# Compressed branch with the token blocks stationary and built by GpSimd, and the rotations' exchanged rows copied inside SBUF

## The chip, the cores and the metric

The kernel runs on one core of a Trainium2 chip. The metric is device microseconds of one execution. A few names are used throughout. PE is TensorE, DVE is VectorE, ACT is ScalarE, POOL is GpSimd and SP is SyncE, which here only issues DMA transfers. SBUF is the on-chip memory of 128 partitions, PSUM the memory into which TensorE writes; GpSimd works in SBUF only here. "Slab" is a 1024 x 256 piece of a weight matrix, "block" its half of 128 output columns.

## What is computed

Two transformer-like blocks over 512 tokens and 1024 channels. The second one has a sparse attention with three branches, a gated linear attention (GLA) and a merge by sigmoid gates. The change touches two places of it: the compressed branch, in which windows of 32 tokens (step 16, so 31 windows) become one key and one value through a small network, and the rotation of queries and keys.

```python
def compress_blocks(kv, pe, w1, w2):          # kv: b, g=2, t=512, d=64
    sub = kv.reshape(b, g, n_sub, CMP_STRIDE, d)
    blocks = jnp.concatenate([sub[:, :, r:r + n_cmp] for r in range(ratio)], axis=3)
    blocks = (blocks + pe).reshape(b, g, n_cmp, CMP_LEN * d)
    return jax.nn.silu(blocks @ w1) @ w2      # 2048 -> 128 -> 64

def partial_rope(x, pos):                     # half = 8 of 64 channels
    x1 = x[..., :half]
    x2 = x[..., half:ROPE_DIM]
    return jnp.concatenate([x1 * cos - x2 * sin, x2 * cos + x1 * sin, x[..., ROPE_DIM:]], axis=-1)
```

The compressed keys then give scores with the unrotated queries, a softmax, and probabilities that are multiplied with the compressed values.

## The kernel before

Everything is written out by hand: each engine has its own list of instructions, and semaphores order them. Activations lie transposed, channels in partitions and the 512 tokens along the free axis. Every large product is done three times at reduced precision (hi*hi, hi*lo, lo*hi), so one block of 128 output channels is 24 products 128x512 (L446). SP loads a slab (w_raw, L343), ACT copies its high part (w_hi, L979), DVE subtracts for the low part (w_lo, L1452); a ring of two slabs is used. PE puts the blocks into four PSUM banks in turn, and block n waits until block n-4 has been emptied. Four other banks, misc 0 to 3, serve small products; `take(b)` waits until the last contents of bank b have been read.

In the stretch that matters here the large products are the eight blocks of the merge gate b, slabs 12 to 15 of the second block's input projection, called block 0 to 7 below. They don't depend on the attention and are put between its small products, so that PE has work while DVE, ACT and POOL finish other steps. ACT empties each with a tanh (gate_out, L1181).

PE's order before: GLA outputs, blocks 0 and 1, mean squares, block 2, spread of the roots (L774), block 3, four rotation products (L783), block 4, two rotation products, block 5, the hidden layer of the compressed branch (L793), block 6, compressed keys (L800) and values (L805), mask and scores (L812, L818), block 7, transposition of the probabilities (L827), then the attention steps, with the blocks of gate a between them.

A rotation takes a constant 128x128 matrix (rot) that exchanges 8 rows with 8 others and turns signs. For each of six tiles (two of keys, four of queries) PE multiplies it, POOL multiplies the tile with cos (L2125), DVE multiplies the PSUM result with sin (L1858) and adds both (L1861). Between the fourth and fifth pair DVE does four ob_lo operations of the GLA output (L1853).

For the hidden layer the windows tile holds, for keys and values and both groups, the raw channels in partitions 0 to 63 (DVE, L1864) and the same shifted by one token in 64 to 127 (ACT, L1298), and the position terms in extra columns (POOL, L2128). Each of 32 products has 128x128 weights as stationary and 66 moving columns at a step of 16 tokens; two of the 66 give the position bias, which DVE adds afterwards (L1871, L1873). ACT does the tanh (L1303), DVE the product (L1877).

ACT's order in the stretch: GLA squares and roots, split of slab 14, four ob_hi, gate_out 0 to 3, four window copies, split of slab 15, two tanh (behind ob_lo), gate_out 4 and 5, split of slab 16, exponentials of the scores. POOL's: two DMA issues for the second weights when the GLA outputs are there (L2118), the cos products, the position columns, a memset, and nothing until the attention steps. A float32 product shows as two records on PE, a large one (reduced precision) as one.

Of the kernel before, what the change touches and what calls it, by code (L numbers as in the profile page):

```python
# [25 lines left out]
P = 128  # L26
# [55 lines left out]
def constants():  # L82
# [9 lines left out]
    rot = np.zeros((P, P), f)  # L92
    for base in (0, HD):
        for k in range(half):
            cos[base + k] = cos[base + half + k] = np.cos(ang[k])
            sin[base + k] = sin[base + half + k] = np.sin(ang[k])
            rot[base + half + k, base + k] = -1.0
            rot[base + k, base + half + k] = 1.0
# [12 lines left out]
    return {"c_recip": recip.reshape(P, -1), "c_cos": cos, "c_sin": sin, "c_rot": rot,  # L111
# [4 lines left out]
def build(nc, a, out):  # L116
# [25 lines left out]
    ROT = at("rot", [P], f32, CB + 3.5)  # L142
# [117 lines left out]
    CONST_DMAS = 5  # L260
# [16 lines left out]
    RS4 = at("gla_roots", [T], f32, R1 + 55)  # L277
# [7 lines left out]
    RAWC = at("kv_cmp_raw", [2, T], f32, R1 + 82)  # L285
    COS, SIN = at("cos", [T], f32, SB + 8), at("sin", [T], f32, R1 + 86)
    OBHI, OBLO = at("ob_hi", [4, T], f32r, R1 + 40), at("ob_lo", [4, T], f32r, R1 + 48)
    Z = at("cmp_windows", [4, T + 32], f32, R1 + 56)
    VBD = at("v_cmp_blocks", [2, 4 * HD], f32, R1 + 82)
    W2 = [at(f"cmp_w2_{i}", [HD], f32, CB + 6 + 0.25 * i) for i in range(2)]  # L290
    HX = [at(f"cmp_hidden{i}", [2 * 32], f32, R1 + 64.5 + 0.25 * i) for i in range(2)]
    HT = [at(f"cmp_tanh{i}", [2 * 32], f32, R1 + 65 + 0.25 * i) for i in range(2)]
    HB = at("cmp_bias", [2], f32, R1 + 65.5)
    KC = at("k_cmp", [32], f32, R1 + 65.625)
# [31 lines left out]
    def _(sp):  # L326
# [31 lines left out]
        for c in range(CC):  # L358
# [3 lines left out]
            if c == 1:  # L362
                for dst, src in [(RECIP[:], a["c_recip"].rearrange("p (g n) -> p g n", n=16)),
                                 (ROT[:], a["c_rot"]), (CAUS32[:], a["c_causal"]),
# [35 lines left out]
        for j, q in enumerate((2, 3, 0, 1)):  # L400
            load(s0 + j, halves(s0 + j, w_2, 0, C2_MG + D + SLAB * q))
# [33 lines left out]
    def _(pe):  # L435
# [350 lines left out]
        pe.wait_ge(S("cmp_loaded"), 16 * 4)  # L786
# [12 lines left out]
        for g in range(2):  # L799
            mm = nc.tensor.matmul(bank[64 * g:64 * g + 64, 0:N_CMP], W2[0][:], HX[0][:, 32 * g:32 * g + N_CMP], start=True, stop=True)  # L800
        mm.then_inc(S("kc_full"), 1)
        pe.wait_ge(S("hidden_ready"), 2)
        bank = take(1)
        for g in range(2):
            mm = nc.tensor.matmul(bank[0:32, 64 * g:64 * g + 64], HX[1][:, 32 * g:32 * g + 32], W2[1][:], start=True, stop=True)  # L805
        mm.then_inc(S("vc_full"), 1)

# [160 lines left out]
    def _(act):  # L968
# [207 lines left out]
        def split(j):  # L1176
            split_hi(s0 + j)
# [118 lines left out]
        for n in range(4):  # L1296
            kv, g = n // 2, n % 2
# [880 lines left out]
```

## Time and profile before

| | us |
|---|---|
| median of 3 runs (1477.80 to 1478.58) | 1477.94 |
| the profiled execution | 1478.09 |
| its span, from the first to the last instruction | 1476.3 |
| PE busy | 1436.4 (97%) |
| DVE busy | 780.8 (53%) |
| ACT busy | 536.6 (36%) |
| POOL busy | 152.0 (10%) |
| mean granted clock of PE, of full speed | 0.984 |

The page gives for each engine the time in which it was busy, and a chain of work followed back from the last instruction. A timeline lists instructions in order of time: start, duration, engine, line of the kernel, operation, output and input tiles, shapes, and how many like it were merged; in brackets the idle time of the engine in front of it. Starts of neighbouring instructions tell more than durations: products overlap in the array, so a large product "lasts" 0.39 us, but the next one starts 0.23 us later.

### The profile page before, as it was taken

How to read it: one execution, taken by the hardware profiler on the slowest of the kernel's cores; microseconds unless marked ns; L12 is line 12 of the kernel's file. 1: busy time of each engine (PE TensorE's matmuls, PEld its weight loads, DVE VectorE, ACT ScalarE, POOL GpSimd, SP SyncE). 2: the span in 40 equal slices, each digit the busy share in tenths (PEclk: the TensorE clock that was granted, in tenths of full speed). 3: DMA queues.
4: the chain of work that ended last, by engine and by line, in shares of the span. 5: the costliest groups of instructions: out<-in, count | busy, mean ns of one | idle time of the engine just before them, and what ended most of it. 6: DMA issues, size and time to landing. Idle time of an engine off the chain costs nothing.

```text
span 1476.3 us, 17308 instructions
## 1 busy us (share of the span) xinstructions
PE 1436.4 (97%) x7234; PEld 1167.2 (79%) x7234; DVE 780.8 (53%) x1029; ACT 536.6 (36%) x752; POOL 152.0 (10%) x125
## 2 busy tenths in 40 slices
PE   7999999899999999989999999999999999999997
PEld 6888688688888888868877687777878888888886
DVE  6998573644233343375683744564445455435533
ACT  5222433543332232254543316662343232212214
POOL 1030023100000000210240202110220000000002
PEclk9999999999999999989999979999999999999999
DMA  7323125013223232323324001102322323233222
GB/s 202 103 86 115 57 86 170 30 58 113 88 88 113 86 107 93 100 86 93 86 66 137 29 29 58 44 16 60 112 91 81 113 86 107 93 91 109 86 86 58
DMA packets 137966, 129.56 MB, mean 88 GB/s; under 512 B 14640, under 2 KB 134464, under 8 KB 137888
## 3 DMA queue, kind: packets, MB, share of 16 engines
q1 hardware_dynamic: 136752, 124.78, 27.2%
q0 software_dynamic: 992, 3.47, 0.8%
q8 instruction: 57, 0.93, 0.3%
q10 hardware_dynamic: 144, 0.20, 0.0%
q14 instruction: 21, 0.17, 0.0%
HBM read 126.34 MB, written 2.10 MB: 87 GB/s over the span
## 4 chain that ended last, share of the span: by engine, by line
PE 95%; ACT 1%; DVE 1%; DMA 1%; POOL 0%; issue 0%; SPq 0%; ACTq 0%
PE gemm L446 76%; PE gemm L847 3%; PE gemm L554 3%; PE misc L874 2%; PE misc L892 1%; PE gemm L593 1%; PE misc L704 1%; PE gemm L649 1%; PE misc L793 1%; DMA w_raw<-in_w_in 1%; PE misc L863 1%; PE gemm L863 1%; PE gemm L604 1%; POOL w_lo L2054 0%; PE misc L502 0%
## 5 line engine op out<-in xcount | busy, mean ns | idle before, releaser
L1452 DVE TENSOR_TENSOR w_lo<-w_raw,w_hi 128x2048 fp32r<-128x2048 f32 (+1 forms) x108 | 245.3, 2271 | 189.2 <-ACT w_hi L979 189.1
L446 PE MATMUL gemm<-h_hi,w_hi 128*128 128x512 f32 x864 | 341.3, 395 | 0.0
L446 PE MATMUL gemm<-h_hi,w_lo 128*128 128x512 f32 x864 | 337.8, 391 | 0.0
L446 PE MATMUL gemm<-h_lo,w_hi 128*128 128x512 f32 x864 | 337.8, 391 | 0.0
L979 ACT ACTIVATE w_hi<-w_raw 128x2048 fp32r<-128x2048 f32 (+1 forms) x113 | 213.8, 1892 | 143.9 <-PE gemm L446 139.5
L446 PEld LDWEIGHTS gemm<-h_hi,w_hi 128*128 128x128 f32 x864 | 163.3, 189 | 37.2 <-issue 2.7
L446 PEld LDWEIGHTS gemm<-h_lo,w_hi 128*128 128x128 f32 x864 | 163.2, 189 | 34.3 <-issue 1.0
L446 PEld LDWEIGHTS gemm<-h_hi,w_lo 128*128 128x128 f32 x864 | 163.1, 189 | 34.3
L446 PE MATMUL gemm<-n_hi,w_hi 128*128 128x512 f32 x352 | 137.4, 390 | 1.6 <-DVE n_lo L1964 1.6
L446 PE MATMUL gemm<-n_lo,w_hi 128*128 128x512 f32 x352 | 137.0, 389 | 0.0
L446 PE MATMUL gemm<-n_hi,w_lo 128*128 128x512 f32 x352 | 137.0, 389 | 0.0
L446 PE MATMUL gemm<-f_hi,w_lo 128*128 128x512 f32 x320 | 124.5, 389 | 0.0
L446 PE MATMUL gemm<-f_hi,w_hi 128*128 128x512 f32 x320 | 124.5, 389 | 0.0
L446 PE MATMUL gemm<-f_lo,w_hi 128*128 128x512 f32 x320 | 124.5, 389 | 0.0
L2086 POOL TENSOR_TENSOR sq_sum<-sq_sum,sq 128x512 f32<-128x512 f32 x28 | 39.0, 1395 | 725.3 <-ACT sq L1378 373.8
L1543 DVE SCALAR_TENSOR_TENSOR conv_out<-v_padded,conv_cols,conv_out 128x512 f32<-128x512 f32 x120 | 89.8, 808 | 0.5
L446 PEld LDWEIGHTS gemm<-n_hi,w_hi 128*128 128x128 f32 x352 | 66.1, 188 | 16.1 <-DVE n_lo L1964 2.3
L446 PEld LDWEIGHTS gemm<-n_hi,w_lo 128*128 128x128 f32 x352 | 66.1, 188 | 13.8
L446 PEld LDWEIGHTS gemm<-n_lo,w_hi 128*128 128x128 f32 x352 | 66.1, 188 | 13.4
L446 PEld LDWEIGHTS gemm<-f_hi,w_hi 128*128 128x128 f32 x320 | 60.1, 188 | 12.5
L446 PEld LDWEIGHTS gemm<-f_hi,w_lo 128*128 128x128 f32 x320 | 60.1, 188 | 12.5
L446 PEld LDWEIGHTS gemm<-f_lo,w_hi 128*128 128x128 f32 x320 | 60.1, 188 | 12.4
(402 smaller groups left out, 1789.9 us busy)
## 6 DMA issues: line engine op xcount, KB each, us to landing
w_raw<-in_w_in SPq DMA_DIRECT2D x62, 512.0 KB, 4.6
w_raw<-in_w_down SPq DMA_DIRECT2D x32, 512.0 KB, 4.1
w_raw<-in_w_up SPq DMA_DIRECT2D x28, 512.0 KB, 4.6
w_raw<-in_w_ffn_gate SPq DMA_DIRECT2D x22, 512.0 KB, 4.5
w_raw<-in_w_ffn_up SPq DMA_DIRECT2D x22, 512.0 KB, 4.5
w_raw<-in_w_ffn_down SPq DMA_DIRECT2D x16, 512.0 KB, 4.2
w_raw<-in_w_o SPq DMA_DIRECT2D x8, 512.0 KB, 4.0
w_raw<-in_w_out SPq DMA_DIRECT2D x8, 512.0 KB, 4.1
```

Source lines behind the costliest of these rows:

```text
L446: mm = nc.tensor.matmul(bank[:], w(s)[:, kt, col0:col0 + P], x(n), start=first, stop=last)
L554: mm = nc.tensor.matmul(G[m % 4][:], wide(w(s0 + j))[:, k, P * b:P * b + P], x[:, k, :], start=k == 0 and n == 0, stop=k == 3 and n == 2)
L593: nc.tensor.matmul(G[(m + b) % 4][:], w(s + b // 2)[:, k, P * (b % 2):P * (b % 2) + P], HHI[:, k, :], start=k == 0 and w is hi_of, stop=False)
L604: mm = nc.tensor.matmul(G[(m + b) % 4][:], hi_of(s + b // 2)[:, k, P * (b % 2):P * (b % 2) + P], HLO[:, k, :], start=False, stop=k == KT - 1)
L649: nc.tensor.matmul(G[m % 4][:], w(s)[:, k, c0:c0 + P], UHI[:, k, :], start=k == 0 and w is hi_of, stop=False)
L847: mm = nc.tensor.matmul(G[bl % 2][:], w(s)[:, kt, P * (bl % 2):P * (bl % 2) + P], y[:, kt, :], start=x % 24 == 0, stop=x % 24 == 23)
L863: nc.tensor.matmul(banks[g][:, 0:w], QT[rows, q, w:w + P], KR[rows, i, 0:w], start=False, stop=False)
L874: mm = nc.tensor.transpose(bank[:, kb * P:(kb + 1) * P], PB[q % 2][:, g, kb * P:(kb + 1) * P], IDENT[:])
L979: nc.scalar.activation(part(hi_of(s), s), part(raw_of(s), s), ACT.Copy).then_inc(S("hi_done"), 1)
L1452: V.tensor_tensor(part(lo_of(s), s), part(raw_of(s), s), f(part(hi_of(s), s)), SUB).then_inc(S("lo_done"), 1)
L1543: ins = V.scalar_tensor_tensor(y, x, w, y, MUL, ADD)
L2086: Q.tensor_tensor(SQA[:], SQA[:], SQ[j % 2][:], ADD).then_inc(S("sq_added"), 1)
```

## The change

Compressed branch. POOL now builds the windows complete, position terms added, as 16 additions of 64 partitions x 8 x 31 elements, straight from the raw keys and values; for half of them input and output lie in other partitions, and the position columns are copied once with the halves exchanged. The windows tile becomes the stationary operand (128x64) and the first weights the moving one (128 columns); keys go to partitions 0 to 63 of one PSUM bank, values to 64 to 127. ACT takes the tanh and DVE the product from that bank once for both. PE then transposes the 128x128 hidden values, ACT copies them to SBUF, and the second weights follow as before. DVE's and ACT's window copies, the bias steps and POOL's position columns go.

Rotation. The matrix, its load and the six products go. SP copies the exchanged rows by eight transfers from SBUF to SBUF (two of 8 partitions x 4 KB for each of two partition groups of the keys, two of 8 x 8 KB for each of the queries), after POOL has set the target tiles to zero; the signs are in the sin table. The transfers stand in SP's list before the load of slab 15. DVE multiplies the copied rows with sin from SBUF.

Order. PE: block 3, block 4, hidden layer, block 5, transposition, a third of block 6, keys and values, a sixth of block 6, scores, the second half of block 6, block 7. DVE does ob_lo after the value blocks instead of between the rotations. POOL does memsets and windows before the cos products; these no longer wait for PE. Some tiles lie at other addresses.

```diff
 SP   for j, q in enumerate((2, 3, 0, 1)):
+            if j == 3:
+                mk = BLOCKS_BEFORE[PH["nsa"][0]]
+                sp.wait_ge(S("swap_zeroed"), 2)
+                for k in (2, 4, 6, 7, 8, 9):
+                    sp.wait_ge(*evac_at(mk + k))
+                for swapped, x in ((RK, KR), (QT, QR)):
+                    for base in (0, HD):
+                        for half in (0, 8):
+                            sp.dma_start(swapped[base + half:base + half + 8, :, :],
+                                         x[base + 8 - half:base + 16 - half, :, :]).then_inc(S("swapped"), 16)
             load(s0 + j, halves(s0 + j, w_2, 0, C2_MG + D + SLAB * q))
...
 PE   gate_block(3)
-        for n in range(6):
-            x = KR[:, n, :] if n < 2 else QR[:, n - 2, :]
-            if n == 4:
-                gate_block(4)
-            nc.tensor.matmul(take(n % 4)[:], ROT[:], x, start=True, stop=True).then_inc(S("rotated"), 1)
-        gate_block(5)
+        gate_block(4)
         pe.wait_ge(S("cmp_loaded"), 16 * 4)
-        pe.wait_ge(S("windows_a"), 4)
-        pe.wait_ge(S("windows_b"), 4)
-        pe.wait_ge(S("positions"), 2)
-        for kv in range(2):
-            bank = take(2 + kv)
-            for j in range(16):
-                mm = nc.tensor.matmul(bank[:, 0:66].rearrange("p (g n) -> p g n", n=33), W1[kv][:, j, :],
-                                      Z[:, 2 * kv:2 * kv + 2, 2 * j:2 * j + T + 1:16], start=j == 0, stop=j == 15)
-            mm.then_inc(S("hidden_full"), 1)
-        gate_block(6)
-        pe.wait_ge(S("hidden_ready"), 1)
+        pe.wait_ge(S("gpsimd_step"), WINDOWS_DONE)
+        bank = take(2)
+        for j in range(16):
+            for kv in range(2):
+                mm = nc.tensor.matmul(bank[64 * kv:64 * kv + 64, 0:P], ZP[:, kv, j, :], W1[kv][:, j, :], start=j == 0, stop=j == 15)
+        mm.then_inc(S("hidden_full"), 1)
+        gate_block(5)
+        misc[2].wait(pe)
+        nc.tensor.transpose(take(3)[:, 0:P], HX[:], IDENT[:]).then_inc(S("hidden_T"), 1)
+        gate_part(6, 0, 8)
+        misc[3].wait(pe)
...
+        gate_part(6, 8, 12)
         misc[0].wait(pe)
...
+        gate_part(6, 12, 24)
         gate_block(7)
 ACT  x in range(4): gate_out(x)
-            A_(Z[64:128, n, 0:T - 1], RAWC[64 * g:64 * g + 64, kv, 1:T], ACT.Copy).then_inc(S("windows_b"), 1)
         split(15)
+        act.wait_ge(S("hidden_full"), 1)
+        A_(HT[:], M[2][:, 0:P], ACT.Tanh, scale=0.5).then_inc(S("hidden_tanh"), 1)
+        act.wait_ge(S("hidden_T"), 1)
+        A_(HXT[:].rearrange("p k n -> p (k n)"), M[3][:, 0:P], ACT.Copy).then_inc(read[3], 1)
         act.wait_ge(S("ob_lo_ready"), 4)
 DVE
+        dve.wait_ge(S("swapped"), 16 * 8)
         for n in range(6):
...
-            V.tensor_tensor(SQ[n % 2][:], M[n % 4][:], SIN[:], MUL).then_inc(read[n % 4], 1)
+            V.tensor_tensor(SQ[n % 2][:], swapped, SIN[:], MUL).then_inc(S("sin_ready"), 1)
...
-            V.tensor_copy(Z[0:64, n, 0:T], RAWC[64 * g:64 * g + 64, kv, :]).then_inc(S("windows_a"), 1)
         split(15)
+        dve.wait_ge(S("hidden_tanh"), 1)
+        V.scalar_tensor_tensor(HX[:], HT[:], 1.0, M[2][:, 0:P], ADD, MUL).then_inc(read[2], 1)
 POOL after the two loads of the second weights
+        Q.memset(RK[:], 0.0).then_inc(S("swap_zeroed"), 1)
+        Q.memset(QT[:], 0.0).then_inc(S("swap_zeroed"), 1)
...
+        for kv in range(2):
+            pool.wait_ge(*evac_at(mk + kv))
+            for g in range(2):
+                rows = slice(64 * g, 64 * g + 64)
+                sub = RAWC[rows, kv, :].rearrange("p (n j h) -> p h j n", j=8, h=2)
+                for h in range(2):
+                    pe_cols = (PE_COLS if g == h else PES)[rows, kv, :]
+                    for jj in range(2):
+                        gstep.wait(pool)
+                        gstep.inc(Q.tensor_tensor(ZP[64 * h:64 * h + 64, kv, 8 * jj:8 * jj + 8, 32 * g:32 * g + N_CMP],
+                                              sub[:, h, :, jj:jj + N_CMP],
+                                              pe_cols[:, 8 * jj:8 * jj + 8].unsqueeze(2).broadcast_to([64, 8, N_CMP]), ADD))
...
-            pool.wait_ge(S("rotated"), n + 1)
+            pool.wait_ge(*evac_at(mk + (2, 4, 6, 7, 8, 9)[n]))
```

## Rows read from the trace of the kernel before

**Rows 1.** The page, chain of work that ended last, by engine.

```profile
PE 95%; ACT 1%; DVE 1%; DMA 1%; POOL 0%; issue 0%; SPq 0%; ACTq 0%
```

**Rows 2.** Timeline of PE, rotation products and the blocks around them.

```profile
831.39 1.88 PE L783 MATMUL misc<-k_rope,rot 128*128 128x512 f32 x4
...
835.05 0.40 PE L446 MATMUL gemm<-h_lo,w_hi 128*128 128x512 f32 x1
...
840.28 1.88 PE L783 MATMUL misc<-q_raw,rot 128*128 128x512 f32 x4
...
842.23 0.40 PE L446 MATMUL gemm<-h_lo,w_hi 128*128 128x512 f32 x1
```

**Rows 3.** Timeline of PE, hidden layer to scores.

```profile
850.16 11.94 PE L793 MATMUL misc<-cmp_windows,cmp_w 128*128 128x66 f32 x64 [2.51 <-issue]
...
862.42 0.63 PE L446 MATMUL gemm<-h_lo,w_hi 128*128 128x512 f32 x1
...
862.85 0.63 PE L446 MATMUL gemm<-h_hi,w_lo 128*128 128x512 f32 x1
...
869.14 0.39 PE L446 MATMUL gemm<-h_hi,w_lo 128*128 128x512 f32 x1
...
870.60 5.04 PE L818 MATMUL misc<-k_cmp,q_raw 64*128 64x31 f32 x64
...
875.57 0.79 PE L446 MATMUL gemm<-h_hi,w_hi 128*128 128x512 f32 x1
```

**Rows 4.** Windows of 1 us: length, PE busy, granted clock, DMA, GB/s.

```profile
849.00:850.00 1.00, 0.00 (x0) 1.00 0.00 0
...
852.00:853.00 1.00, 1.00 (x9) 0.68 0.06 16
...
873.00:874.00 1.00, 1.00 (x14) 0.50 0.07 16
```

**Rows 5.** Line 745 (min/median/max ns, first and last start); timeline of PE behind it.

```profile
L745 PE MATMUL misc<-v_gla,k_tokens x24: 272/273/323, 792.7 to 794.0; 128*64 128x128 f32 x24
...
794.20 0.50 PE L446 MATMUL gemm<-h_hi,w_hi 128*128 128x512 f32 x1
```

**Rows 6.** Timeline of ACT, emptying of blocks 0 to 3.

```profile
832.11 2.04 ACT L1181 ACTIVATE gate_tanh<-gemm 128x512 f32<-128x512 f32 x4
```

**Rows 7.** Timeline of DVE, slab split, gla_out, key rotation, ob_lo, score maximum.

```profile
823.29 2.23 DVE L1452 TENSOR_TENSOR w_lo<-w_raw,w_hi 128x2048 fp32r<-128x2048 f32 x1
...
830.84 0.69 DVE L1847 TENSOR_TENSOR gla_out<-gla_out,gla_gate 128x512 f32<-128x512 f32 x1
...
833.87 1.74 DVE L1861 TENSOR_TENSOR k_rope<-sq,h_now 128x512 f32<-128x512 f32 x1 [0.66 <-POOL h_now L2125]
...
840.91 4.67 DVE L1853 SCALAR_TENSOR_TENSOR ob_lo<-gla_out,ob_hi 128x512 fp32r<-128x512 f32 x4
...
875.66 0.69 DVE L1890 TENSOR_REDUCE cmp_max<-misc 128x16 f32<-128x512 f32 x1 [3.70 <-PE misc L818]
```

**Rows 8.** Timeline of POOL; then POOL's groups by form (total us, mean ns).

```profile
807.93 0.55 POOL L2118 DMA_DIRECT2D cmp_w<-in_cmp_v_w  x1
...
832.57 2.50 POOL L2125 TENSOR_TENSOR h_now<-k_rope,cos 128x512 f32<-128x512 f32 x2 [24.09 <-PE misc L783]
...
L2054 POOL TENSOR_TENSOR w_lo<-w_raw,w_hi 128x256 fp32r<-128x256 f32 x8 | 6.5, 846 | 14.0 <-ACT w_hi L979 14.0
...
L2100 POOL MEMSET gla_attn<- 128x2048 f32 x1 | 1.8, 1812 | 39.4 <-PE gemm L446 39.4
```

**Rows 9.** Timeline of DVE and PE, end of the scaling, transpositions.

```profile
881.34 1.29 DVE L1909 TENSOR_TENSOR p_cmp<-p_cmp,cmp_factor 128x512 f32<-128x512 f32 x2
...
883.04 1.03 PE L827 MATMUL misc<-ident,p_cmp 128*128 128x128 f32 x8
```

**Rows 10.** Timeline of SP; the page's DMA issues (count, KB, us to landing).

```profile
12.54 0.46 SPq L367 DMA_DIRECT2D rot<-in_c_rot  x1
...
w_raw<-in_w_in SPq DMA_DIRECT2D x62, 512.0 KB, 4.6
```

More of the change, by code:

```diff
@@ L95, in constants @@
             cos[base + k] = cos[base + half + k] = np.cos(ang[k])
[L96 to L98 removed]
+            sin[base + k], sin[base + half + k] = -np.sin(ang[k]), np.sin(ang[k])
     causal = np.where(np.arange(P)[None, :] <= np.arange(P)[:, None], 0.0, -1e30).astype(f)
@@ L796, in _, with gate_part @@
-        gate_block(6)
-        pe.wait_ge(S("hidden_ready"), 1)
+        gate_block(4)
+        pe.wait_ge(S("cmp_loaded"), 16 * 4)
+        pe.wait_ge(S("gpsimd_step"), WINDOWS_DONE)
[4 more added lines that the diff above has]
+        mm.then_inc(S("hidden_full"), 1)
+        gate_block(5)
+        def gate_part(x, first, last):
+            s = s0 + 12 + x // 2
+            m, b = BLOCKS_BEFORE[s] + x % 2, x % 2
+            if first == 0:
+                pe.wait_ge(S("lo_done"), s + 1)
+                pe.wait_ge(evac[m % 4], m // 4 + 1)
+            for n in range(first, last):
+                w, y = ((hi_of, HHI), (hi_of, HLO), (lo_of, HHI))[n % 3]
+                mm = nc.tensor.matmul(G[m % 4][:], w(s)[:, n // 3, P * b:P * b + P], y[:, n // 3, :], start=n == 0, stop=n == 23)
+            if last == 24:
+                mm.then_inc(S("block_full"), 1)
@@ L803, in _ @@
         bank = take(1)
         for g in range(2):
-            mm = nc.tensor.matmul(bank[0:32, 64 * g:64 * g + 64], HX[1][:, 32 * g:32 * g + 32], W2[1][:], start=True, stop=True)
+            mm = nc.tensor.matmul(bank[0:32, 64 * g:64 * g + 64], HXT[:, 2 + g, :], W2[1][:], start=True, stop=True)
         mm.then_inc(S("vc_full"), 1)
+        gate_part(6, 8, 12)
         misc[0].wait(pe)
@@ L1295, in _ @@
             gate_out(x)
-        for n in range(4):
-            kv, g = n // 2, n % 2
-            A_(Z[64:128, n, 0:T - 1], RAWC[64 * g:64 * g + 64, kv, 1:T], ACT.Copy).then_inc(S("windows_b"), 1)
         split(15)
+        act.wait_ge(S("hidden_full"), 1)
+        A_(HT[:], M[2][:, 0:P], ACT.Tanh, scale=0.5).then_inc(S("hidden_tanh"), 1)
+        act.wait_ge(S("hidden_T"), 1)
+        A_(HXT[:].rearrange("p k n -> p (k n)"), M[3][:, 0:P], ACT.Copy).then_inc(read[3], 1)
         act.wait_ge(S("ob_lo_ready"), 4)
-        for kv in range(2):
-            act.wait_ge(read[2 + kv], 15)
-            A_(HT[kv][:], HX[kv][:], ACT.Tanh, scale=0.5).then_inc(S("hidden_tanh"), 1)
         gate_out(4)
@@ L1307, in _ @@
         for g in range(2):
-            act.wait_ge(read[2 + g], 16)
+            act.wait_ge(read[2 + g], 15)
             x = PC[:, :, 4 * g:4 * g + 4, :]
@@ L1848, in _ @@
         dve.wait_ge(S("rope_loaded"), 32)
+        dve.wait_ge(S("swapped"), 16 * 8)
         for n in range(6):
[L1850 to L1855 removed]
+            dst, swapped = (KR[:, n, :], RK[:, n, :]) if n < 2 else (QT[:, n - 2, :], QT[:, n - 2, :])
             if n >= 2:
                 dve.wait_ge(S("ropes_ready"), n - 1)
[L1858 removed]
+            V.tensor_tensor(SQ[n % 2][:], swapped, SIN[:], MUL).then_inc(S("sin_ready"), 1)
             dve.wait_ge(S("cos_ready"), n + 1)
[L1860 removed]
+            dve.wait_ge(S("sin_ready"), n + 1)
             V.tensor_tensor(dst, SQ[n % 2][:], HS[n % 2][:], ADD).then_inc(S("ropes_ready"), 1)
[L1862 to L1877 removed]
+        split(15)
+        dve.wait_ge(S("hidden_tanh"), 1)
+        V.scalar_tensor_tensor(HX[:], HT[:], 1.0, M[2][:, 0:P], ADD, MUL).then_inc(read[2], 1)
         dve.wait_ge(S("kc_full"), 1)
@@ L1885, in _ @@
         ins.then_inc(read[1], 1)
+        for hd in range(GLA_H):
+            dve.wait_ge(S("ob_hi_ready"), hd + 1)
+            V.scalar_tensor_tensor(OBLO[:, hd, :], OSB[:, hd, :], 0.5, f(OBHI[:, hd, :]), MUL, SUB).then_inc(S("ob_lo_ready"), 1)
         for g in range(2):
@@ L2118, in _ @@
             pool.dma_start(W2[i][:], a[n][0]).then_inc(S("cmp_loaded"), 16)
+        Q.memset(RK[:], 0.0).then_inc(S("swap_zeroed"), 1)
+        Q.memset(QT[:], 0.0).then_inc(S("swap_zeroed"), 1)
+        pe0 = ROW0["cmp_pe_k_2"]
+        PE_COLS = PV[:, pe0:pe0 + 32].rearrange("p (k j) -> p k j", j=16)
+        for i in range(2):
+            gstep.inc(Q.tensor_copy(PES[64 * i:64 * i + 64], PE_COLS[64 - 64 * i:128 - 64 * i]))
+            gstep.wait(pool)
+        gstep.inc(Q.memset(ZP[:].rearrange("p k j (g n) -> p (k j g) n", n=32)[:, :, N_CMP:32], 0.0))
+        mk = BLOCKS_BEFORE[PH["small"][0] + 7]
+        for kv in range(2):
[6 more added lines that the diff above has]
+                    for jj in range(2):
+                        gstep.wait(pool)
+                        gstep.inc(Q.tensor_tensor(ZP[64 * h:64 * h + 64, kv, 8 * jj:8 * jj + 8, 32 * g:32 * g + N_CMP],
+                                              sub[:, h, :, jj:jj + N_CMP],
+                                              pe_cols[:, 8 * jj:8 * jj + 8].unsqueeze(2).broadcast_to([64, 8, N_CMP]), ADD))
+        assert gstep.n == WINDOWS_DONE
+        gstep.wait(pool)
         pool.wait_ge(S("rope_loaded"), 32)
```

52 lines of the change are left out of this document (11 added, 41 removed).

## The prediction

> **What bounds the kernel now.** I read the page's chain of work first: TensorE (PE) makes 95% of it [rows 1]. So time goes away only where PE itself does less, waits less, or runs at a higher clock. Then I read PE's timeline over the stretch that the change rewrites, about 831 to 885 us, because there the small products stand between the large 128x512 ones. Four things in it cost PE time.
>
> - *Rotation products.* Four start at 831.39. The second large product behind them starts at 835.05; with one pitch of 0.23 us taken off (23 products between 835.05 and 840.28: 0.227 each), block 4 begins at 834.82. That is 3.43 us. The last two start at 840.28, and the same reading gives 842.00, so 1.72 us. Together 5.15 us [rows 2].
> - *A wait.* PE stands idle for 2.51 us before the hidden-layer products at 850.16 [rows 3]. It waits for the windows, which DVE and ACT copy after the rotations.
> - *Hidden-layer products.* They run from 850.16 until block 6 begins at 861.99 (862.42 less one pitch of 0.43): 11.83 us for 64 records. After the idle time the granted clock is still 1.00, but at 852 it falls to 0.50, from 2.4 to 1.2 GHz [rows 3, 4].
> - *Block 6 at the low clock.* Its 24 large products need 861.99 to 869.37, 7.4 us, against 24 x 0.227 = 5.45 us at the high clock: 1.9 us [rows 3].
>
> Sum of what stands there: 5.15 + 2.51 + 11.83 + 1.9 = 21.4 us. During the score products behind them the clock falls again (0.50 at 873) [rows 3, 4].
>
> **Removed and added on PE.** The six rotation products go: -5.15. The hidden layer swaps its operands. Before, 128 columns were loaded as stationary and only 66 moved. Now the window block (64 columns) is stationary, the weights (128 columns) move, and keys and values alternate between the two column halves. This form is in the trace: the state update, 128x64 stationary, 128x128 moving, alternating halves, 24 records whose starts lie 1.3 us apart, 0.056 us each [rows 5]. The new layer has as many records as the old, 64: 64 x 0.056 + 0.2 for its ends = **3.8 us**, -8.0 against 11.83. Bounds: 3.6, and 7.2 if the halves don't overlap or the clock is low. The 128x128 transposition of the hidden values is two records of a form whose eight take 1.03 us: 0.26, I take 0.3 [rows 9]. Transposition and the separate key/value products make two more changes between small and large products; each costs about 0.1 before and 0.1 behind (the first large product after the state update lasts 0.50, not 0.39 [rows 5]): +0.4. Cutting block 6 into parts costs nothing else.
>
> **The wait that comes back.** Block 4 writes the PSUM bank of block 0, which ACT must first empty. ACT does so behind the fourth ob_hi, in the first of four activations that start at 832.11 and take 2.04; it is done at about 832.7 [rows 6]. PE is through with block 3 at 831.39. Until now the rotation products covered this 1.3 us; the change takes the cover away. It is also lengthened. ob_hi waits for DVE's four pairs of gla_out operations, the last of which ends at 831.45, and GpSimd (POOL), idle in that stretch before, now works there. The trace shows what that does: a DVE addition of two SBUF operands at 833.87 lasts 1.74 us while POOL runs two multiplications from 832.57 to 835.07; without POOL the same kind lasts 0.69 [rows 7, 8]. One engine waits for the other's instruction.
>
> The Trainium skill says the same (SBUF — State Buffer, Who interferes with whom): a DVE instruction with two SBUF inputs and a GpSimd instruction that reads SBUF exclude each other for the whole instruction. By that rule the trace agrees, 1.74 against 0.69.
>
> When does POOL work? It is free at 808.5, after its last DMA issue [rows 8]. Two memsets, 1024 and 2048 columns: 0.95 + 1.81 us; two small copies and a small memset some 0.8, an estimate: the windows begin at 812.1. They are 16 additions of 64 x 248 elements. No strided POOL operation is in the trace. A 128x256 subtraction averages 0.85 us, a 128x512 multiplication 1.25 (two in 2.50) [rows 8]. Scaling the latter by elements gives 0.60 as one bound, taking it whole 1.25 as the other; the 256 columns are nearest, 0.83, and with 0.07 (an estimate) between dependent ones 0.9. 16 x 0.9 = 14.4, so 826.5, and the w_lo operation on DVE at 823.29 (2.23 us, two SBUF inputs) pushes it to **828.7** [rows 7]. PE wants the windows only at about 840, so they are not waited for; 11 us of cover, gone at 1.5 us an operation. But their last ones, and the two cosine multiplications behind them (1.25 each), fall on DVE's gla_out pairs: three or four of four products wait some 0.5 us, **+1.9** (bounds 0.3 and 3). The stall of PE before block 4 is then 1.3 + 1.9 = **3.2 us** (1.6 to 4.3).
>
> The Trainium skill has a rule that speaks against building windows there (GPSIMD Engine Reference, Performance pitfalls for Q7 kernels): reads of SBUF whose step is over 8 bytes take about 2.9 instead of 1.9 cycles per element; these read with a step of 64 bytes. No run yet shows it. By it an operation would come near my upper bound rather than 0.83; it is a rival below.
>
> **Edits with no term.** DVE's six rotations now take the swapped rows from SBUF, so both operations of each pair meet POOL's cosines: 12 x 0.65 of DVE and 4 x 1.25 of POOL one after another, 12.8 us from 833.4, to 846.2. The split of slab 15 (2.23) and the hidden product then end at 848.7; PE asks for it after block 5, at about 849.4. Cover 0.7 us, nothing charged, up to 2 in the range. ACT loses four window copies, DVE four and the bias steps. The four ob_lo operations (4.67 us with POOL beside them [rows 7]) move behind the value blocks: 4 x 0.65 from 853.9 to 856.6, before the scores end at about 859. ACT waits for them before it empties blocks 4 and 5 and splits slab 16, some 3 us together, so until 859.7, just before the scores want it at 860.6. From the start of the score maximum at 875.66 to the end of the scaling at 882.6 DVE and ACT need 7.0 us; PE came at 883.04 [rows 7, 9]. Now half of block 6 stands there too, 2.7 us more, so this wait stays covered.
>
> SP issues the eight swap transfers before its load of slab 15. It waits for POOL's memsets at 811.3; at 0.46 us an issue [rows 10] it is done at 815. The load comes some 10 us later; it lands 4.6 us after issue, by 820, and ACT splits it only behind the four activations, after 834 [rows 6, 10]. The swaps are small; even 7 us to landing is 822, against 833. One constant load less at the start changes nothing that PE waits for.
>
> **The sum.** Gone: 21.4. Back: 3.8 + 3.2 + 0.3 + 0.4 = 7.7. Net -13.7. The profiled execution took 1478.09 us, its span 1476.3. 1476.3 - 13.7 = 1462.6, and 1.8 around it: **1464.4 us**. (The median of the runs lies 0.15 below the profiled one.) About 0.2% is what a measurement of this kernel can tell from no change, 3 us.
>
> **The rivals.**
>
> *The clock falls after the new stall.* For it: 2.5 us of idle and thin products behind it were followed by 0.50 [rows 3, 4]. Against it: here dense blocks stand on both sides, and at 849, after idle time, the clock was still 1.00. Price: low from some 835 for about 3.5 us, as block 6's low stretch lasted some 4: half of it, +1.7: 1466.1; twice that for two such stretches. Chance 0.24.
>
> *POOL's window operations take 1.25 us each*, as if of full width. Windows at 836, cosines until 838.5: all four gla_out products collide (stall 3.8), the rotations on DVE end 2 us later and the transposition waits 1.3: +1.9, 1466.3. Chance 0.14.
>
> *The clock holds through the scores*, because large products now stand before and between. The scores' 64 records then go at the pitch of their first part. They took 4.97 us, the second half of that at 0.50, so about 1.5 of it is the clock, and block 7 started at the low clock like block 6 (1.9): up to 3.4 us less, 1461.0; with a short stall 1459.5. Chance 0.18.
>
> *The halves don't overlap:* the hidden layer takes 7.2: +3.4, 1467.8. Against it [rows 5]. Chance 0.04.
>
> *Slower than before.* POOL is the bound: windows read with a step of 16 elements into other partitions, a form that no row shows. PE waits at 840 - 812.1 = 28 us, 1.75 an operation; at 2.6 it waits 13.7 us and the gain is gone; at 3.0 the windows are done at 861, 21 us late: 1485. This would be three to four times the nearest row. Chance 0.04 slower, 0.03 even.
>
> **Chances and range.** Forecast 0.33. Every case but the last is faster. Faster 0.93, within 0.2% 0.03, slower 0.04. The range: from 1460 (clock held) to 1469 (clock fallen twice, or POOL slow and clock fallen); it holds eight in ten.
>
> **What would show it.** Right: no rotation products; hidden-layer records at a pitch near 0.056 us and clock 1.00; PE idle about 3 us before block 4 and released by ACT's emptying of the bank; none before the hidden layer; gla_out products on DVE that last over 1 us; POOL additions of 0.7 to 1.0 us ending near 829; block 6 at 0.23 us a product. Wrong: PE idle before the hidden layer (POOL late), before the transposition (DVE late) or before the score transpositions (ACT or DVE late behind ob_lo); or 0.50 in the clock between 835 and 850.

## The result, and the profile after

The changed kernel takes **1462.4 us** (median of four runs, 1459.22 to 1463.72) where the kernel before takes 1478.14 beside it (four runs, 1477.80 to 1478.58): a ratio of 0.9892, 95% interval 0.9877 to 0.9907. It is faster, by 15.7 us. The profiled execution took 1461.57 us; its span is 1459.8, against 1476.3.

The timeline of TensorE (PE) over the stretch, to be laid beside [rows 2, 3]; columns are start, us, engine, line, what it does, count, and in brackets the idle time ahead of it with its releaser:

```profile
830.71 0.77 PE L453 MATMUL gemm<-h_hi,w_hi 128*128 128x512 f32 x1 [2.17 <-ACT gate_tanh L1197]
831.27 0.63 PE L453 MATMUL gemm<-h_lo,w_hi 128*128 128x512 f32 x1
...
833.83 0.49 PE L453 MATMUL gemm<-h_lo,w_hi 128*128 128x512 f32 x1
...
837.92 3.71 PE L792 MATMUL misc<-cmp_w,cmp_windows 128*64 128x128 f32 x64
841.57 0.50 PE L453 MATMUL gemm<-h_hi,w_hi 128*128 128x512 f32 x1
...
847.15 0.27 PE L810 MATMUL misc<-ident,cmp_hidden 128*128 128x128 f32 x1
847.17 0.48 PE L805 MATMUL gemm<-h_hi,w_hi 128*128 128x512 f32 x1
...
851.33 4.18 PE L833 MATMUL misc<-k_cmp,q_raw 64*128 64x31 f32 x64
855.44 0.79 PE L805 MATMUL gemm<-h_hi,w_hi 128*128 128x512 f32 x1
856.03 0.63 PE L805 MATMUL gemm<-h_lo,w_hi 128*128 128x512 f32 x1
...
866.49 1.03 PE L843 MATMUL misc<-ident,p_cmp 128*128 128x128 f32 x8
```

There are no rotation products and no idle time ahead of the hidden layer. That layer takes 3.65 us (837.92 to 841.57) in place of 11.83. A new wait of 2.17 us stands before block 4. Behind it, and again behind the scores, the large products last 0.63 us, which is a pitch of 0.43: the low clock. Windows of 1 us and one of 0.1 us (length, busy share of PE, PEld, DVE, ACT and POOL, PE's granted clock, DMA), as in [rows 4]:

```profile
829.00:830.00 1.00, 0.00 (x0) 0.00 (x0) 1.00 (x2) 0.55 (x2) 0.00 (x0) 1.00 0.00 0
...
830.60:830.70 0.10, 0.00 (x0) 0.03 (x1) 0.10 (x1) 0.10 (x1) 0.00 (x0) 0.58 0.00 0
...
831.00:832.00 1.00, 1.00 (x3) 0.81 (x3) 0.90 (x2) 1.00 (x4) 1.00 (x1) 0.50 0.00 0
...
838.00:839.00 1.00, 1.00 (x20) 1.00 (x22) 0.90 (x2) 0.00 (x0) 1.00 (x1) 1.00 0.00 0
...
854.00:855.00 1.00, 1.00 (x18) 1.00 (x16) 0.20 (x1) 0.76 (x2) 0.00 (x0) 0.76 0.00 0
```

In 829:830 PE does nothing and the record still shows 1.00. The fall to 0.50 (1.2 GHz) comes at about 830.62, while PE still waits, just ahead of its first product at 830.71. It is back at 2.4 GHz for the hidden layer. The other engines, as in [rows 6 to 9], from the timelines of GpSimd (POOL), ScalarE (ACT), VectorE (DVE):

```profile
809.15 1.54 POOL L2137 TENSOR_TENSOR cmp_windows<-kv_cmp_raw,param_cols 64x248 f32<-64x248 f32 x2
810.77 3.15 POOL L2137 TENSOR_TENSOR cmp_windows<-kv_cmp_raw,cmp_positions_swapped 64x248 f32<-64x248 f32 x4
...
820.57 3.49 POOL L2137 TENSOR_TENSOR cmp_windows<-kv_cmp_raw,param_cols 64x248 f32<-64x248 f32 x2
824.14 3.33 POOL L2148 TENSOR_TENSOR h_now<-k_rope,cos 128x512 f32<-128x512 f32 x2
```

```profile
829.45 0.63 ACT L1308 ACTIVATE ob_hi<-gla_out 128x512 fp32r<-128x512 f32 x1 [0.75 <-DVE gla_out L1861]
829.98 2.04 ACT L1197 ACTIVATE gate_tanh<-gemm 128x512 f32<-128x512 f32 x4
...
854.24 1.09 ACT L1197 ACTIVATE gate_tanh<-gemm 128x512 f32<-128x512 f32 x2 [6.50 <-DVE ob_lo L1885]
```

```profile
823.68 0.93 DVE L1861 TENSOR_TENSOR gla_out<-gla_out,gla_gate 128x512 f32<-128x512 f32 x1
...
825.30 1.01 DVE L1861 TENSOR_TENSOR gla_out<-gla_out,gla_gate 128x512 f32<-128x512 f32 x1
...
828.72 0.69 DVE L1861 TENSOR_TENSOR gla_out<-gla_out,gla_gate 128x512 f32<-128x512 f32 x1
...
831.52 1.59 DVE L1871 TENSOR_TENSOR k_rope<-sq,h_now 128x512 f32<-128x512 f32 x1
...
843.51 0.28 DVE L1874 SCALAR_TENSOR_TENSOR cmp_hidden<-cmp_tanh,misc 128x128 f32<-128x128 f32 x1
```

The four products of gla_out last 0.93, 1.01, 1.02 and 0.69 us: three are lengthened while POOL works. The last ob_hi therefore starts at 829.45, ACT empties block 0's bank behind it, and PE gets its bank. The hidden product is made by 843.8, 3.3 us before PE wants it at 847.1.

**The account.** From DVE's reciprocal before the stretch (start 820.02 before, 817.00 after) to the transpositions of the probabilities (883.04 [rows 9], 866.49), 63.02 us became 49.49: **-13.5**. The other **-3.0** of the span stood in the trace before the stretch began, in code that the change touches only by one constant load less at the start. It comes up bit by bit: DVE's slab splits start 0.18 us earlier at the kernel's start, 0.70 at 311 us, 1.46 at 656 and 3.04 at 690. The last step is one stretch of low clock, which the kernel before has and this one hasn't. The first 1.46 us are the executions' and hardly the change's: in a second profile of the changed kernel (the last experiment below) the split near 656 starts at 656.09, before at 655.96. Windows of 664 to 668 us, first before, then after:

```profile
664.00:668.00 4.00, 4.00 (x12) 3.09 (x11) 4.00 (x8) 3.94 (x5) 0.00 (x0) 0.58 0.00 0
```

```profile
664.00:668.00 4.00, 4.00 (x19) 3.33 (x18) 4.00 (x7) 2.75 (x3) 0.00 (x0) 1.00 0.00 0
```

### The profile page after: what moved, and what is told of

Read it like the earlier page. It is cut to its first block, busy times and chain, and to the rows that moved or that the text cites. A ratio compares the mean times of both kernels' runs of the same rounds, so it can differ in the third digit from the quotient of the medians.

```text
span 1459.8 us, 17295 instructions
## 1 busy us (share of the span) xinstructions
PE 1420.1 (97%) x7223; PEld 1153.3 (79%) x7223; DVE 778.1 (53%) x1018; ACT 534.3 (37%) x748; POOL 170.4 (12%) x144
## 4 chain that ended last, share of the span: by engine, by line
PE 95%; ACT 1%; DVE 1%; DMA 1%; POOL 0%; issue 0%; SPq 0%; ACTq 0%
PE gemm L453 75%; PE gemm L863 3%; PE gemm L561 3%; PE misc L890 2%; PE misc L908 1%; PE gemm L600 1%; PE misc L711 1%; PE gemm L656 1%; DMA w_raw<-in_w_in 1%; PE gemm L805 1%; PE misc L879 1%; PE gemm L879 1%; PE gemm L611 1%; POOL w_lo L2054 0%; PE gemm L667 0%; ACT w_hi L995 0%
## 5 line engine op out<-in xcount | busy, mean ns | idle before, releaser
L453 PE MATMUL gemm<-h_hi,w_hi 128*128 128x512 f32 x856 | 336.7, 393 | 2.2 <-ACT gate_tanh L1197 2.2
L453 PE MATMUL gemm<-h_lo,w_hi 128*128 128x512 f32 x856 | 333.9, 390 | 0.0
L453 PE MATMUL gemm<-h_hi,w_lo 128*128 128x512 f32 x856 | 333.7, 390 | 0.0
L453 PEld LDWEIGHTS gemm<-f_lo,w_hi 128*128 128x128 f32 x320 | 60.1, 188 | 12.5
```

Source lines behind the costliest of these rows:

```text
L453: mm = nc.tensor.matmul(bank[:], w(s)[:, kt, col0:col0 + P], x(n), start=first, stop=last)
```

## The experiments

All times are medians; the kernel before was run beside each. Two theories stood for the stretch. *Cover:* the rotation products only filled a time in which PE must wait for ACT anyway, so the gain is all in the hidden layer; what is given back is the wait before block 4, made of blocks that end early and of DVE's products beside POOL. *Clock:* part of what is given back is the lower clock that follows a wait or thin products.

### Each half of the change alone

The rotation half on the kernel before, and the compressed half alone on the changed kernel:

```diff
  # rotation only: swaps by DMA inside SBUF; the windows and the hidden layer stay as before
-        for n in range(6):
-            x = KR[:, n, :] if n < 2 else QR[:, n - 2, :]
-            if n == 4:
-                gate_block(4)
-            nc.tensor.matmul(take(n % 4)[:], ROT[:], x, start=True, stop=True).then_inc(S("rotated"), 1)
+        gate_block(4)
...
  # compressed only: the changed kernel with these products put back
```

> The kernel before with the rotation part of the change alone (swap transfers, no rotation products; windows, hidden layer and ob_lo as before). If my reading of the change holds, the 5.15 us of rotation products come back as waits: block 4 waits some 1.3 to 2.3 us for ACT to empty its bank, and the idle time before the hidden layer (2.5 us before) grows to 4 to 6, because the window copies on DVE stand behind its own chain and not behind PE. So 1476 to 1479 us. If PE's work were all that counts (rival), 1478.1 - 5.15 = 1473.

Measured: 1476.67 us (1472.05 to 1477.55, 12 runs), beside 1476.09 for the kernel before (1474.79 to 1483.58, 17 runs); ratio 0.9992 (0.9981 to 1.0003). That is no gain clear of noise, and 2.8 us at most. Its PE timeline shows where 5.15 us went:

```profile
832.21 0.47 PE L453 MATMUL gemm<-h_hi,w_hi 128*128 128x512 f32 x1 [1.28 <-ACT gate_tanh L1183]
...
847.30 13.10 PE L795 MATMUL misc<-cmp_windows,cmp_w 128*128 128x66 f32 x64 [3.97 <-DVE cmp_windows L1866]
```

The uncovered wait is 1.28 us (forecast for it: 1.3). The wait for the windows grew from 2.51 to 3.97, since DVE and ACT set it and PE only came sooner. The hidden layer, 11.94 before [rows 3], now takes 13.10: the granted clock falls 0.9 us after its first product, where before it fell after 2.2. These are 3.9 of the 5.15 us. With the low clock in the blocks behind, 4.5 of them come back: from DVE's reciprocal to the transpositions of the probabilities this profile has 62.33 us, the kernel before 63.02.

> The changed kernel with the rotation done by TensorE as before (products between blocks 3 and 4, two more behind block 4), so the compressed part of the change alone. My theory: the rotation products cover the emptying of the bank, so no stall before block 4 and no fall of the clock there; against the changed kernel +5.15 for the products, -2.3 for the stall, -1.4 for the low clock behind it: +1.5, 1464. The rival, that the two parts add up and the stall is something else: +5.15, 1467.5.

Measured: 1462.31 us (1459.23 to 1463.13), ratio 0.9897 (0.9883 to 0.9910): the whole change's time within the spread. There is no wait before block 4, and the hidden layer is as short:

```profile
840.79 3.71 PE L790 MATMUL misc<-cmp_w,cmp_windows 128*64 128x128 f32 x64
...
844.44 0.50 PE L447 MATMUL gemm<-h_hi,w_hi 128*128 128x512 f32 x1
```

So the compressed half is the gain, as far as the times can tell. Beside it the rotation half's 5.15 us come back mostly as 2.33 us of wait (2.17 in the row, 2.33 from pitch to pitch) and some 1.4 of low clock behind it. From DVE's reciprocal (818.72 here) to the end of the hidden layer the profiles have 25.72 us here and 24.57 in the changed kernel. So 1.15 us of the rotation half stay there, and 0.7 in the kernel before: about 1 us, less than the times can show. Behind the hidden layer this execution makes them up, for it has only 7 large products at the low clock behind the scores, the changed kernel 12.5.

### Taking the wait before block 4 away, in two ways

```diff
  # ACT: each gate's half right behind its ob_hi
             A_(OBHI[:, hd, :], OSB[:, hd, :], ACT.Copy, scale=0.5).then_inc(S("ob_hi_ready"), 1)
-
-        for x in range(4):
-            gate_out(x)
+            gate_out(hd)
```

> The changed kernel, but ACT empties block n right behind the n-th ob_hi instead of behind all four. Bank 0 is then free at about 826, before block 3 ends at 828.4. My theory: the stall of 2.3 us before block 4 goes, and with it the low clock behind it (1.4): 1458.7 (1457.5 to 1460). Rival: another thing is late next (the windows, or the hidden product on DVE), the stall only moves: 1462.

Measured: 1458.44 us (1457.67 to 1460.14), ratio 0.9876 (0.9863 to 0.9888), as the theory asks. Beside it the compressed half alone took 1462.31. PE has no idle time before block 4, the clock of 828:832 is 1.00, and a small wait appears further on:

```profile
834.27 3.71 PE L792 MATMUL misc<-cmp_w,cmp_windows 128*64 128x128 f32 x64
...
844.15 0.33 PE L810 MATMUL misc<-ident,cmp_hidden 128*128 128x128 f32 x1 [0.50 <-DVE cmp_hidden L1872]
```

```diff
  # PE: the hidden layer ahead of block 4
-        gate_block(4)
         ...hidden layer...
+        gate_block(4)
```

> The changed kernel, but the hidden layer stands before block 4 instead of behind it. The windows were ready at 824.1, block 3 ends at 828.4, so its 3.7 us lie where PE was idle. My theory: stall and low clock go, same as with ACT's order changed: 1458.7 (1457.5 to 1460). Rival, the clock: the hidden layer's form counts as thin for it, as the old form did, and it falls to 0.50 behind the layer: 1460.5.

Measured: 1458.8 us (1458.42 to 1459.17), ratio 0.9877 (0.9863 to 0.9892). The hidden layer fills the place in which PE waited, since the windows are long done:

```profile
828.58 3.71 PE L791 MATMUL misc<-cmp_w,cmp_windows 128*64 128x128 f32 x64
...
843.95 0.33 PE L810 MATMUL misc<-ident,cmp_hidden 128*128 128x128 f32 x1 [0.55 <-DVE cmp_hidden L1874]
```

Two edits on different engines, with the same result, name the cause: it is that wait, with the clock behind it. The profiles say the same, in which the clock behind the scores fell in all three: the stretch from DVE's reciprocal to the transpositions takes 46.21 and 46.28 us, in the changed kernel 49.49. That is 3.2 to 3.3 less, which is 2.33 + 1.4 less the new wait of 0.5. By the times both are 3.5 to 4 us faster than the compressed half beside them.

### What the wait is made of

```diff
  # POOL, ahead of its cosines
+        pool.wait_ge(S("ob_ready"), GLA_H)
         for n in range(6):
```

> The changed kernel with one wait more: GpSimd's first two cosine products wait until VectorE has made all four rows' products of the gated layer, so that nothing of GpSimd's runs beside them. Theory (the wait before block 4 is made of TensorE's four blocks ending earlier, 1.3 us, and of VectorE's products lengthened by GpSimd's two cosines, 0.9 us): the products take 0.69 us each, TensorE's idle time ahead of block 4 falls from 2.17 to about 1.3 us, the rotations end up to 1 us later, which nothing waits for (TensorE asks for the hidden product 3.3 us after it is made), and the time falls by 0.9 us, or by up to 2.3 if the clock now holds behind the shorter wait. Rival (the lengthening comes from something else, such as the order of ScalarE's copies): the wait stays above 2.0 us and the time is unchanged.

Measured: 1460.51 us (1458.67 to 1461.13), ratio 0.9881 (0.9866 to 0.9895); the changed kernel again, beside it, 1461.6. The rows:

```profile
832.12 0.47 PE L453 MATMUL gemm<-h_hi,w_hi 128*128 128x512 f32 x1 [1.53 <-ACT gate_tanh L1197]
...
847.41 0.33 PE L810 MATMUL misc<-ident,cmp_hidden 128*128 128x128 f32 x1 [0.26 <-DVE cmp_hidden L1874]
```

The second and third product of gla_out fall to 0.69 us; the first stays at 0.94, beside POOL's last window operation. The wait falls from 2.17 to 1.53, to 1.3 plus the one collision left. So the collisions with the cosines cost 0.6 of it and the last window operation 0.25. One expectation missed: the rotations end 1.5 us later, not up to 1, PE comes some 2 us sooner for the shorter wait and the clock, and so the transposition waits 0.26. The time fell by 1.1 us, within the spread of both.

This execution also shows what the clock is worth. The record shows 1.00 in the whole stretch, which takes 44.62 us for 49.49. The wait is 0.64 of that; nearly all the rest is clock. The window of 852 to 864 us, in the changed kernel and here:

```profile
852.00:864.00 12.00, 12.00 (x82) 10.18 (x81) 10.33 (x21) 4.15 (x5) 0.00 (x0) 0.72 0.01 1
```

```profile
852.00:864.00 12.00, 12.00 (x102) 10.47 (x101) 10.71 (x22) 4.04 (x5) 0.00 (x0) 1.00 0.01 1
```

### The hidden layer's form

```diff
-        for j in range(16):
-            for kv in range(2):
+        for kv in range(2):
+            for j in range(16):
                 mm = nc.tensor.matmul(bank[64 * kv:64 * kv + 64, 0:P], ZP[:, kv, j, :], W1[kv][:, j, :], start=j == 0, stop=j == 15)
```

> The changed kernel, with the 32 hidden-layer products in another order: all 16 of the keys (column half 0 to 63), then all 16 of the values (half 64 to 127), instead of alternating. Same work. My theory, that the pitch of 0.056 us comes from two halves that overlap: no overlap, 64 records at about 0.11 us, 7.0 instead of 3.7: +3.3, 1465.7. Rival, that a narrow stationary block is enough: 0.056 stays, 1462.4.

Measured: 1463.48 us (1462.15 to 1465.44), ratio 0.9907 (0.9893 to 0.9920); only 1.1 above, where 3.3 were expected. The row shows the effect:

```profile
837.30 6.82 PE L792 MATMUL misc<-cmp_w,cmp_windows 128*64 128x128 f32 x64
```

The next block starts at 844.05. That is 6.75 us, 0.105 a record, against 3.65 and 0.057: the same products follow each other at half the pitch when they alternate between the two column halves. The 3.1 us are there. In this profile only 7 large products behind the scores stand at the low clock, against 12.5 in the changed kernel's, and the scores are 0.2 us shorter. That gives 1.6 us back: the stretch takes 50.95 us for 49.49.

```diff
-                mm = nc.tensor.matmul(bank[64 * kv:64 * kv + 64, 0:P], ZP[:, kv, j, :], W1[kv][:, j, :], ...)
+                mm = nc.tensor.matmul(bank[:, 64 * kv:64 * kv + 64], W1[kv][:, j, :], ZP[:, kv, j, :], ...)
-        nc.tensor.transpose(take(3)[:, 0:P], HX[:], IDENT[:]).then_inc(S("hidden_T"), 1)   # and ACT's copy behind it
```

> The changed kernel with the operands in their old roles: the 128x128 weights stationary, POOL's 64 window columns moving, hence no transposition and no copy of it by ACT. My theory: 64 records at 0.107 us (the old layer's pitch while the clock was high) = 6.8 instead of 3.7, less 0.1 for the transposition: +3.0, 1465.4, and up to 3 more if the clock falls in it. So of the 8.1 us by which the hidden layer became shorter some 5 belong to the idle time and the clock, and 3 to the roles. Rival: the roles are worth nothing, 1462.4; or all of it: 1470.

Measured: 1463.55 us (1459.64 to 1464.29), ratio 0.9908 (0.9892 to 0.9923). The profiled run happens to be the fastest of its four:

```profile
830.36 0.47 PE L453 MATMUL gemm<-h_hi,w_hi 128*128 128x512 f32 x1 [2.11 <-ACT gate_tanh L1195]
...
835.88 7.25 PE L792 MATMUL misc<-cmp_windows,cmp_w 128*128 128x64 f32 x64
...
852.57 3.76 PE L831 MATMUL misc<-k_cmp,q_raw 64*128 64x31 f32 x64
```

The next block starts at 842.94. So with 128 stationary columns 64 moving ones cost 7.06 us, 0.110 a record, at the high clock, nearly twice the alternating form. The kernel before had 66 moving columns and mostly the low clock: by subtraction some 4.8 of its 11.83 us were the clock and 3.4 the form, an estimate. This execution also shows the same wait of 2.11 us with no low clock behind it (the first product lasts 0.47; 1.00 over 830:834). Its scores take 3.76 us with block 7 at 1.00: the rival in which the clock holds, as also with the cosines later and with POOL's windows doubled. So it came in three of the eleven profiles that have the compressed half. Its low time, 1459.64, is that clock; the other three runs took 1463.22 to 1464.29.

### POOL's cover

```diff
+                        for twice in range(2):
                         gstep.inc(Q.tensor_tensor(ZP[...], sub[:, h, :, jj:jj + N_CMP], pe_cols[...]..., ADD))
-WINDOWS_DONE = (0 + 1 + 2 + 3) + 3 + 16
+WINDOWS_DONE = (0 + 1 + 2 + 3) + 3 + 32
```

> The changed kernel with each of POOL's 16 window additions done twice (same values). They would end at about 837, just before PE wants them at 837.9. If only the windows' own deadline counts (the 11 to 13 us of cover of the prediction): +0.5 at most, 1463. My theory: POOL's cosines behind them come at 837 to 840, DVE's rotations end near 850 instead of 841.3, the split of slab 15 and the hidden product at 853; PE wants that at 847.1: idle for 6 us before the transposition, the clock falls behind it: +6 to +8, 1469 to 1471.

Measured: 1470.97 us (1468.71 to 1472.43, 5 runs), ratio 0.9955 (0.9943 to 0.9968). Doubling POOL's work costs half of the gain:

```profile
828.34 1.28 DVE L1861 TENSOR_TENSOR gla_out<-gla_out,gla_gate 128x512 f32<-128x512 f32 x1
...
834.79 0.47 PE L453 MATMUL gemm<-h_hi,w_hi 128*128 128x512 f32 x1 [3.09 <-ACT gate_tanh L1197]
...
835.71 0.63 PE L453 MATMUL gemm<-h_hi,w_hi 128*128 128x512 f32 x1
...
857.86 0.48 PE L810 MATMUL misc<-ident,cmp_hidden 128*128 128x128 f32 x1 [6.45 <-DVE cmp_hidden L1874]
```

The windows themselves are done at 841.7 and the hidden layer starts at 842.04 without a wait. What comes late is the chain behind them: cosines, rotations, hidden product. The wait before block 4 grows by 0.9, since all four products of gla_out now meet a window operation: they last 0.81, 1.28, 1.27 and 1.23 us, 1.8 us more than 4 x 0.69, and 1.3 + 1.8 is the 3.09 of the row. The low clock comes back too, from the third product of block 4 on. So POOL's point of decision is the transposition, not the hidden layer. In the changed kernel two covers stand ahead of it: the 3.3 us by which the hidden product is early, and 3.5 us for which POOL, done with its first two cosines, waits for DVE. The doubled windows end 14.5 us later in the stretch and the hidden product comes 10.9 later, 3.6 less. An estimate from these: 6.8 us over 16 operations is 0.4, so the cover is gone at some 1.2 us an operation, where it takes 0.8.

### The scores, and the small wait that was left

```diff
  # on top of the interleaved kernel: two large products behind each of the first three groups of 16 score records
-        gate_part(6, 12, 24)
+            if t < TT - 1:
+                gate_part(6, 12 + 2 * t, 14 + 2 * t)
+        gate_part(6, 18, 24)
```

> The kernel with ACT's order changed (1458.4), and the four groups of 16 score records each followed by two large products of block 6, which stood behind all of them. My theory: the clock falls in and behind the scores because their records are thin; with large products between them it may hold: 3.4 us less for scores and blocks 6 and 7, +0.6 for six more changes of form: 1455.6. If it falls all the same: 1459.

Measured: 1458.41 us (1456.11 to 1461.62), ratio 0.9873 (0.9857 to 0.9889): no change. The first three groups take 1.08 us each at 1.00, the fourth 1.92, and 855:862 is at 0.51 all the same. Spacing doesn't keep the fall away. It comes 4.5 us after the first score product, behind 48 records; without the spacing it came after 3.0 us (848.42 to 851.42), some 51 records in.

```diff
  # on top of the interleaved kernel, DVE
-        split(15)
         dve.wait_ge(S("hidden_tanh"), 1)
         V.scalar_tensor_tensor(HX[:], HT[:], 1.0, M[2][:, 0:P], ADD, MUL).then_inc(read[2], 1)
+        split(15)
```

> The interleaved kernel (ScalarE makes each gate's half right behind its copy) with VectorE's steps exchanged in one place: the product of the hidden layer comes before the low half of slab 15, which took 2.29 us just ahead of it. Theory (the 0.50 us that TensorE waits for that product before the transposition is this queueing): the wait goes and the time is 0.5 us below the interleaved kernel's 1458.4, about 1457.9. Rival (the product would have waited for ScalarE's tanh, or block 7 now waits for slab 15): the wait stays or a new one takes its place, 1458.4 or more.

Measured: 1459.31 us (1456.01 to 1460.69), ratio 0.9871 (0.9857 to 0.9886): no gain; the rival's case. PE's transposition waits no more, but one row on:

```profile
846.59 0.50 PE L805 MATMUL gemm<-h_hi,w_hi 128*128 128x512 f32 x1 [0.44 <-DVE w_lo L1464]
```

So the order only chose which of the two steps PE waits for: DVE's queue as a whole is late.

### The changed kernel again

> The changed kernel itself, again, in the job of the other two, to set its time and the spread between its executions beside theirs. The theory that most of its spread is where the clock falls, and not a wait, asks for a trace whose waits are those of the first profile (2.17 us before block 4, none before the transposition) whatever its time between 1459 and 1464; the rival (a wait whose length varies) asks for a longer wait in a longer run.

Measured: 1461.6 us (1459.67 to 1463.01), ratio 0.9886 (0.9869 to 0.9902). The profile is of the longest of these runs, 1463.01, 1.4 us over the first profile:

```profile
832.22 0.77 PE L453 MATMUL gemm<-h_hi,w_hi 128*128 128x512 f32 x1 [2.11 <-ACT gate_tanh L1197]
...
839.41 3.71 PE L792 MATMUL misc<-cmp_w,cmp_windows 128*64 128x128 f32 x64
...
852.82 4.19 PE L833 MATMUL misc<-k_cmp,q_raw 64*128 64x31 f32 x64
```

The rows of the stretch are those of the first profile, 1.5 us later. The difference is there by 656 us (DVE's splits: +0.03 at the start, +0.77 at 311, +1.59 at 656), and it stays 1.4 to 1.6 to the end. It is the clock in other stretches, as the theory asked: the mean granted clock is 0.97 over 150:200 and 0.91 over 600:656 us, in the first profile 1.00 and 0.94.

## Why the prediction was right, point by point

- **The hidden layer.** Forecast 3.8 us by the pitch of [rows 5], measured 3.65. Confirmed by the experiment without alternation, 6.75. The rival in which the halves don't overlap is out.
- **The wait that comes back.** Its place, its releaser and its uncovered part hold: 1.28 us in the rotation half alone, forecast 1.3. Its second part was mis-sized: +1.9 forecast, +0.9 measured. Three products meet POOL, as forecast, but each is lengthened by 0.24 to 0.33 us and not by some 0.5. With POOL's windows doubled three are lengthened by 0.5 to 0.6 and one by 0.12, so 0.5 is what a product loses to a dense row of window operations; here those were over at 824.06, soon after the first product had started, and the other two met the cosines.
- **POOL's windows.** Forecast 0.9 us an operation; 14 of them take 0.81 each (809.15 to 820.5), and DVE's w_lo at 820.27 holds up the last two by 1.9, near the forecast push of 2.2. The start agrees: 809.15, on a trace that is 3.0 us early, for 812.1. So POOL came 1.6 us earlier than forecast and the rival of 1.25 us is out.
- **The rule on strided reads.** An operation of 248 elements takes 0.73 us (median of the sixteen, each 0.8 behind the last), 3.0 ns an element; the dense 128x256 subtraction of [rows 8] takes 3.3. So reading with a step of 64 bytes shows no extra cost here, against the nearest dense row, which is another operation on 128 partitions. The Trainium skill (GPSIMD Engine Reference, Performance pitfalls for Q7 kernels) has half as much again per element for such reads. No row here shows it, and the measurement decides.
- **Who waits for whom.** The rotations' additions last 1.58 to 1.59 us beside a cosine and 0.69 without one, as in [rows 7]. By the exclusion that the Trainium skill states (SBUF — State Buffer, Who interferes with whom) the trace agrees, with these numbers.
- **Edits with no term.** No wait before the transposition, right, though the cover was 3.3 us and not 0.7: DVE's six rotations take 12.1 us, not 12.8, and start earlier. No wait behind ob_lo, right: DVE and ACT need 7.0 us behind the scores (855.53 to 862.5) and PE comes at 866.49. The swaps land in time, though SP's issues follow each other at 0.7 us, and the forecast had 0.46.
- **The clock.** The forecast case had no fall behind the new wait. In the profiled run it fell: seven products at 0.43 us, 7 x 0.2 = 1.4. That is the first rival, priced at +1.7. It fell in both profiles of the changed kernel, with the halves not alternating (wait 2.15) and with the windows doubled (3.09), and not with the weights stationary (2.11), with the cosines later (1.53) nor in the rotation half alone (1.28). What decides it at one and the same wait is open. Behind the scores it stayed low for 12.5 products where block 7 before had some 9; the scores in turn took 4.11 us to the next block, not 4.97.
- **The sum.** Back: 3.65 + 2.33 + 1.4 + 0.1 for the transposition, and 0.4 by subtraction for form changes and the clock around the scores: 7.9, against 7.7. In the stretch -13.5, forecast -13.7. Two errors of about 1 us, the collisions and the clock, cancel; that the sum came so close is luck.
- **What no step had.** 1464.4 is 2 us above the median. They are not from the stretch, where the sum missed by 0.2: they are in code ahead of it, where the executions differ, in part by the low clock. The dip at 664 us is in the traces of the kernel before, of the rotation half and in four of the eleven traces with the compressed half, and not in the other seven. Whether the change makes it rarer is open. The range, 1460 to 1469, was laid around the stretch alone. It holds the median, but one of the four runs took 1459.22, so its lower end ought to have reached further down for this.

## What to carry to other kernels

Ask of each product that you take off the bound engine what it covered: 5.15 us of rotations went, and about 1 us was gained, too little for the times to show, because the same time was needed by ScalarE and VectorE. What did pay was a form in which 64 small products alternate between column halves (0.057 us for 0.105 to 0.110) and stand where the clock is high, without a wait of 2.5 us ahead of them. When such a cover goes, put other ready work in its place (the hidden layer before block 4), or empty banks in the order in which they are wanted: about 3 us more, for a move of one line. Near the end of such a hunt a gain of a few microseconds must be read from the stretch in the trace, since the clock in unchanged code moves single runs by as much.

## What the runs showed that was not expected

- The granted clock falls after thin work and not only after idle time: at 854 us PE is busy for the whole microsecond with 64x31 products and gets 0.76, then 0.50. And the same wait (2.11 us) is followed by 0.50 in one execution and 1.00 in another.
- The granted clock doesn't fall at a fixed place of a wait: in the changed kernel it falls 0.1 us before PE's first product behind the wait (830.62). In the kernel before it falls 2.2 us after the first product of the hidden layer, and in the 6.45 us of waiting with the windows doubled it falls in the middle (0.71 over 855:857), 2 us before PE is at work again.
- SP issues the swaps' transfers inside SBUF at a distance of 0.67 to 0.73 us (eight from 808.21 to 813.78), where the constant loads follow each other at 0.5 (that of rot is 0.46 long [rows 10]).
- What a DVE operation loses to one of POOL's is no constant: products of gla_out lost 0.24 to 0.33 us in the changed kernel, 0.12 to 0.59 with POOL's windows doubled, and the additions of the rotations beside a cosine 0.9. The rows fit one reading, which was not tested by itself: a product loses what POOL's operation under way has left to do when it wants to start.
